# Weight splits in two-tile pieces, gate gemms over all levels, and smaller moves in a model of three blocks

## The reference, cut to what matters

```python
for l in range(2):                       # first model, 16 meta + 512 tokens, width 1024
    h = h + 0.5 * swiglu(rms_norm(h, ffn1_norm[l]), ffn1_w_gu[l], ffn1_w_down[l])
    u = rms_norm(h, mix_norm[l])
    c_q, c_kv, k_pe, hq, hf, hi, hg, ga, gb = split_cols(u @ w_in[l], IN_SPLITS)
    y_a = mla(c_q, c_kv, k_pe, ...) @ w_proj_attn[l]       # 8 heads, causal, with rope
    y_b = hgrn2(hq, hf, hi, hg, lbs[l], hg_norm[l]) @ w_proj_rec[l]   # 4 heads, gated recurrence
    merged = sigmoid(ga) * y_a + sigmoid(gb) * y_b
    h = h + merged @ w_out[l]
    h = h + 0.5 * swiglu(rms_norm(h, ffn2_norm[l]), ffn2_w_gu[l], ffn2_w_down[l])
x = rms_norm(h, final_norm)[:, 16:]
# second model, one layer, 512 tokens
u, q, k, v, qi, ki, wi, gates = split(rms(x) @ w_in_2)
y_ssm = s5(u)                            # complex diagonal recurrence, gelu, sigmoid gate
y_att = attention over the 256 keys that the indexer picks (top_k of qi, ki, wi)
x = x + (sigmoid(g_ssm) * (y_ssm @ w_proj_ssm) + sigmoid(g_att) * (y_att @ w_proj_attn)) @ w_out
x = x + (silu(h2 @ w_gate) * (h2 @ w_up)) @ w_down       # h2 = rms(x)
```

## Time and profile before

| | us |
|---|---|
| median of 3 runs | 3305.68 |
| lowest, highest | 3302.39, 3307.8 |
| profiled execution, its own time | 3303.59 |
| span of that execution's trace | 3301.8 |
| PE busy | 3218.9 (97%) |
| DVE, ACT, POOL busy | 1745.8, 1120.4, 1450.2 |

### The profile page before, as it was taken

One profiled execution on the slowest core, in us unless ns is written; L12 is line 12 of the kernel. 1 busy time (PEld: TensorE's weight loads), 2 busy tenths in 40 slices (PEclk: granted clock), 3 DMA queues, 4 the chain that ended last, 5 costly groups with the idle time before them and its releaser, 6 DMA issues.

```text
span 3301.8 us, 55446 instructions
## 1 busy us (share of the span) xinstructions
PE 3218.9 (97%) x21512; PEld 2916.4 (88%) x21512; DVE 1745.8 (53%) x2634; ACT 1120.4 (34%) x1590; POOL 1450.2 (44%) x661
## 2 busy tenths in 40 slices
PE   8999999999999999999999999999999999999999
PEld 7999988899999999999999888788888776788888
DVE  7363553477563546543662477633235678655434
ACT  4232433322342334332343222332324434243322
POOL 3564542122445655555642222444465442245555
PEclk9999999999999999999999999999999999999999
DMA  4333322133333333333332123333333433233333
GB/s 129 90 95 96 92 70 52 39 94 115 96 90 96 92 91 93 91 92 96 90 85 58 46 81 118 96 95 105 93 94 91 109 95 118 64 90 89 102 89 102
DMA packets 544860, 298.89 MB, mean 91 GB/s; under 512 B 23280, under 2 KB 528624, under 8 KB 544560
## 3 DMA queue, kind: packets, MB, share of 16 engines
q1 hardware_dynamic: 514128, 258.77, 27.6%
q10 hardware_dynamic: 30560, 37.72, 3.6%
HBM read 278.36 MB, written 16.91 MB: 89 GB/s over the span
## 4 chain that ended last, share of the span: by engine, by line
PE 61%; issue 25%; POOL 8%; DVE 4%; ACT 1%; DMA 1%; ACTq 0%; POOLq 0%; DVEq 0%; SPq 0%
PE pair L663 28%; PE pair L661 22%; PE aux L721 10%; POOL wl L526 6%; POOL SL L542 2%; DMA raw<-w_ffn_gate 0%; DVE tmp L1754 0%; PE aux L690 0%; ACTq L1513 0%; DVE negt L2244 0%; DVE top L2243 0%; DVE R L1702 0%; DVE R L1697 0%; DVE al L1757 0%; DVE R L2339 0%
## 5 line engine op out<-in xcount | busy, mean ns | idle before, releaser
L526 POOL TENSOR_TENSOR wl<-raw,wh 128x1024 fp32r<-128x1024 f32 (+4 forms) x513 | 1156.6, 2258 | 1812.5 <-ACT wh L1161 1610.5
L1161 ACT ACTIVATE wh<-raw 128x1024 fp32r<-128x1024 f32 (+4 forms) x513 | 490.2, 958 | 477.0 <-DMA raw<-ffn_w_down 152.8
L663 PE MATMUL pair<-xh,wh 128*128 128x264 f32 x2208 | 348.1, 291 | 18.9 <-DVE xl L1647 14.4
L1657 DVE SCALAR_TENSOR_TENSOR hT<-pair,hT 128x528 f32 (+3 forms) x144 | 100.8, 700 | 452.9 <-PE pair L663 258.9
L663 PE MATMUL pair<-xl,wh 128*128 128x264 f32 x2208 | 333.6, 285 | 0.0
L663 PE MATMUL pair<-xh,wl 128*128 128x264 f32 x2208 | 328.3, 285 | 0.0
L663 PEld LDWEIGHTS pair<-xh,wh 128*128 128x128 f32 x2208 | 295.5, 190 | 27.7 <-ACT wh L1161 9.3
L663 PEld LDWEIGHTS pair<-xl,wh 128*128 128x128 f32 x2208 | 295.3, 189 | 0.0
L663 PEld LDWEIGHTS pair<-xh,wl 128*128 128x128 f32 x2208 | 292.9, 189 | 0.0
L661 PE MATMUL pair<-xh,wh 128*128 128x512 f32 x920 | 255.5, 403 | 0.0
L661 PE MATMUL pair<-xl,wh 128*128 128x512 f32 x920 | 248.8, 395 | 0.0
(11 more groups left out here) (396 smaller groups left out, 5373.2 us busy)
## 6 DMA issues: line engine op xcount, KB each, us to landing
raw<-ffn_w_gu SPq DMA_DIRECT2D x176, 512.0 KB, 3.8
raw<-w_in SPq DMA_DIRECT2D x103, 512.0 KB, 3.9
raw<-ffn_w_down SPq DMA_DIRECT2D x64, 512.0 KB, 4.0
raw<-ffn_w_down SPq DMA_DIRECT2D x32, 384.0 KB, 3.5
raw<-w_out SPq DMA_DIRECT2D x24, 512.0 KB, 4.0
raw<-w_ffn_gate SPq DMA_DIRECT2D x22, 512.0 KB, 3.8
raw<-w_ffn_up SPq DMA_DIRECT2D x22, 512.0 KB, 3.9
gate_scratch<-gst ACTq DMA_DIRECT2D x32, 256.0 KB, 2.5
```

Source lines behind the costliest of these rows:

```text
L526: nc.gpsimd.tensor_tensor(wl[:, k % SPL, 0:n], raw[:, k % SPL, 0:n], wh[:, k % SPL, 0:n].bitcast(F32), ALU.subtract).then_inc(S["split_don ...
L663: mm = nc.tensor.matmul(pp[:, h, 0:th], wk, x[:, kk, t0 + h * th:t0 + (h + 1) * th], start=first, stop=last)
L1161: nc.scalar.activation(wh[:, k % SPL, 0:n], raw[:, k % SPL, 0:n], ACT.Copy).then_inc(S["split_hi"], 1)
L1657: v.scalar_tensor_tensor(halves(hm, T // 2), psum_pair(k, T // 2), factor, halves(hm, T // 2), ALU.mult, ALU.add).then_inc(S["evacuated"], 1)
```

## The change

It does seven things, on all engines. (1) GpSimd makes the low halves two k-tiles (256 columns) at a time in the gates, the projections, the output gemm and the second model's gemms, with one semaphore increment at the end as before. (2) The token sums of the FFNs are made a slot sooner: tile 0, then 1 and 2 in one slot, then 3. (3) The gate gemms stand at the levels of the table GATE_AT; its first entry is done in the tail of the attention (`first_gate`), its last after level 35, and with it the evacuation, the sigmoid, the store and the way back of all gates. (4) v turns begin behind two k-tiles of the first hgrn unit, and the tiles 2 to 4 stand within that unit; their banks are swapped; the rope copies are split over two slots. (5) The angles of chunk 0 stand ahead of the first gates on ScalarE and DVE, and three picks there are left to the attention's rounds. (6) The halves of the second attention's output are made for the tokens 0 to 383 at rounds 27 and 28, for the last 128 at the end. (7) In `v_turns` a wait for the probabilities' copies moves behind tile 0.

```diff
+        GATE_AT = (0, 3, 5, 7, 9, 11, 14, 16, 18, 20, 23, 25, 27, 30, 32, 35)
...
-            def split(l, k, kt, i=0):
-                n = kt * P
+            def split(l, k, kt, i=0, kp=None):
+
+                kp = kt if kp is None else kp
                 pool.wait_ge(S["split_hi"], U(l, k, i) + 1)
-                nc.gpsimd.tensor_tensor(wl[:, k % SPL, 0:n], raw[:, k % SPL, 0:n], wh[:, k % SPL, 0:n].bitcast(F32),
-                                        ALU.subtract).then_inc(S["split_done"], 1)
-
-            def run(l, k, kts, turns):
+                for k0 in range(0, kt, kp):
+                    n = slice(k0 * P, (k0 + kp) * P)
+                    ins = nc.gpsimd.tensor_tensor(wl[:, k % SPL, n], raw[:, k % SPL, n], wh[:, k % SPL, n].bitcast(F32), ALU.subtract)
+                ins.then_inc(S["split_done"], 1)
+
+            def run(l, k, kts, turns, kp=None):
                 with pool.Fori(0, turns) as i:
                     for j in range(4):
-                        split(l, k + j, kts[j], i)
+                        split(l, k + j, kts[j], i, kp)
...
-                run(l, U_GATE, [KD] * 4, 4)
-                run(l, U_PROJ, [4] * 4, 4)
-                run(l, U_WO, [KD] * 4, 2)
+                run(l, U_GATE, [KD] * 4, 4, 2)
+                run(l, U_PROJ, [4] * 4, 4, 2)
+                run(l, U_WO, [KD] * 4, 2, 2)
...
-            def v_turns(src, base):
-
-                for i, (st, sz) in enumerate(TT1):
+            def v_turns(src, base, tiles=range(len(TT1)), free=None):
+
+                for i in tiles:
+                    st, sz = TT1[i]
                     r = base + i
                     if i >= 2:
                         pe.wait_ge(S["vt_copied"], r - 1)
+                    if i == 1 and free is not None:
+                        pe.wait_ge(*free)
                     for j in range(4):
-                        mm = nc.tensor.transpose(bank[2 + i % 2][0:sz, j * 128:(j + 1) * 128], src(j, st, sz), ident)
+                        mm = nc.tensor.transpose(bank[3 - i % 2][0:sz, j * 128:(j + 1) * 128], src(j, st, sz), ident)
                     mm.then_inc(S["vt_done"], 1)
...
+                def v_tiles(*tiles):
+                    v_turns(lambda j, st, sz: vT[j][:, st:st + sz], l * 10, tiles)
+
+                def hg_slice(n, slot):
+                    if n == 1 and slot == 0:
+                        pe.wait_ge(S["vt_copied"], l * 10 + 5)
+                    for k, kt, kk in PLANS[l].parts[n][slot]:
+                        if n == slot == 0:
+                            if kk < 2:
+                                continue
+                            if kk in (4, 6):
+                                v_tiles(kk // 2)
+                        gemm(l, k, kt, (xh, xl), th, part=(kk,), alone=True)
+                        if n == slot == 0 and kk == KD - 1:
+                            v_tiles(4)
+                            pe.wait_ge(S["vt_copied"], l * 10 + 4)
+                t0, T = real(l)
+
+                def first_gate(x):
+                    if x == 0:
+                        pe.wait_ge(S["evacuated"], U(l, U_GATE) + PAIRS)
+                        gemm(l, U_GATE, KD, (xh, xl), T // 2, t0=t0)
                 pe.wait_ge(S["evacuated"], U(l, U_HG) + PAIRS)
-                v_turns(lambda j, st, sz: vT[j][:, st:st + sz], l * 10)
-
-                def hg_slice(n, slot):
-                    for k, kt, kk in PLANS[l].parts[n][slot]:
-                        gemm(l, k, kt, (xh, xl), th, part=(kk,), alone=True)
+                for kk in range(2):
+                    gemm(l, U_HG, KD, (xh, xl), th, part=(kk,), alone=True)
+                v_tiles(0, 1)
                 pe.wait_ge(S["rope_copied"], 3 * l + 3)
-                pe.wait_ge(S["vt_copied"], l * 10 + 5)
                 attention(at1[l], lambda h, st, sz: qT[:, h, st:st + sz], lambda h, c0, c1: kT[:, h, c0:c1],
                           lambda x, kn, h: vtok[0:kn, x, h * 64:h * 64 + 64], mask1,
-                          lambda n: hg_slice(n, 0), lambda n: hg_slice(n, 1))
-                pe.wait_ge(S["evacuated"], U(l, U_GATE) + PAIRS)
-                pe.wait_ge(at1[l].sem["pt_copied"], at1[l].n + at1[l].groups)
-                v_turns(lambda j, st, sz: hgv[j][:, st:st + sz], l * 10 + 5)
-
-                t0, T = real(l)
+                          lambda n: hg_slice(n, 0), lambda n: hg_slice(n, 1), first_gate)
+                v_turns(lambda j, st, sz: hgv[j][:, st:st + sz], l * 10 + 5, free=(at1[l].sem["pt_copied"], at1[l].n + at1[l].groups))
+
                 lv = 0
                 for i, (st, sz) in enumerate(TT1):
                     nl = sz.bit_length()
...
                                 lt, rt, n = kd[m % 2][:, h, 0:sz], qd[m % 2][:, h, 0:sz // 2], sz // 2
                             mm = nc.tensor.matmul(bank[lv % 2][0:sz, h * 128:h * 128 + n], lt, rt, start=True, stop=True)
                         mm.then_inc(S["lv_done"], 1)
-                        if lv == 0 or lv >= 3 and lv % 2 == 1 and lv // 2 < 2 * KD:
-                            gemm(l, U_GATE + lv // 2, KD, (xh, xl), T // 2, t0=t0)
+                        if lv in GATE_AT[1:]:
+                            gemm(l, U_GATE + GATE_AT.index(lv), KD, (xh, xl), T // 2, t0=t0)
...
-                            if early:
-                                kk = 2 * i + j
+                            for kk in ((0,), (1, 2), (3,), ())[2 * i + j] if early else ():
                                 w_thi(fs, kk, T // 2)
...
-                    for n in (1, 2) if j == 11 else ():
+                    for n in (j - 10,) if j in (11, 12) else ():
...
-                    while g < 2 * KD and 2 * g + 3 < lv:
+                    while g < 2 * KD - 1 and GATE_AT[g + 1] < lv:
                         gate(l, U_GATE, g, T, l)
                         g += 1
-                    if i == len(TT1) - 1:
-                        assert g == 2 * KD
-                        gates_back(l, U_GATE, T, gates2 if T == SEQ else gates1, l)
                     if i < len(TT1) - 1:
                         act.wait_ge(S["kht_done"], l * 4 + i + 1)
                         nc.scalar.activation(khT[0:sz, :, :], bank[3][0:sz, :].rearrange("p (h k) -> p h k", h=HG),
...
                         act.wait_ge(S["kq_ready"], l * 5 + i + 1)
                         for j in range(4):
                             nc.scalar.activation(ah[:, j, t0:T1], oT[:, j, t0:T1], ACT.Copy).then_inc(S["oth"], 1)
+                        assert g == 2 * KD - 1
+                        gate(l, U_GATE, g, T, l)
+                        gates_back(l, U_GATE, T, gates2 if T == SEQ else gates1, l)
...
+            angles(0)
             act.wait_ge(S["n2_ss"], 6)
             nc.scalar.activation(rq, bank[2][:, 0:32], ACT.Sqrt, bias=eps[:, 2:3]).then_inc(S["n2_rms"], 1)
             gates(0, EARLY)
-            angles(0)
...
+                if n == 27:
+                    act.wait_ge(at2.sem["pt_copied"], 29)
+                    nc.scalar.activation(ah[:, 0:4, 0:384], oT[:, :, 0:384], ACT.Copy).then_inc(S["oth"], 2)
...
-            for j in range(4):
-                nc.scalar.activation(ah[:, j, 0:SEQ], oT[:, j, 0:SEQ], ACT.Copy).then_inc(S["oth"], 1)
+            nc.scalar.activation(ah[:, 0:4, 384:SEQ], oT[:, :, 384:SEQ], ACT.Copy).then_inc(S["oth"], 2)
...
-                            w_tlo(fs, j - 1, th)
+                            w_tlo(fs, (0, 2, 3)[j - 1], th)
+                        if j == 1:
+                            w_tokens(fs, 1, T, own)
                         evac(l, k + 2 * j + 1, tm(US, T), rstd[:, 0:T], th)
                         dve.wait_ge(S["evacuated"], U(l, k + 2 * j + 1) + 1 + PAIRS)
                         activated(fi * FT + j, j)
-                        w_tokens(fs, j, T, own)
-                    if early:
-                        w_tlo(fs, 3, th)
+                        if j == 1:
+                            w_tlo(fs, 1, th)
+                        if j < 3:
+                            w_tokens(fs, (0, 2, 3)[j], T, own)
...
+                def v_copies(*tiles):
+                    for i in tiles:
+                        st, sz = TT1[i]
+                        dve.wait_ge(S["vt_done"], l * 10 + i + 1)
+                        v.tensor_copy(vtok[0:sz, i, :], bank[3 - i % 2][0:sz, :]).then_inc(S["vt_copied"], 1)
+                v_copies(0, 1)
...
-                    if lv >= 3 and lv % 2 == 1 and lv // 2 - 1 < 2 * KD:
-                        gate(l, U_GATE, lv // 2 - 1, T, l, rstd[:, t0:T1])
+                    if lv in GATE_AT[1:]:
+                        gate(l, U_GATE, GATE_AT.index(lv) - 1, T, l, rstd[:, t0:T1])
...
+                        gate(l, U_GATE, 2 * KD - 1, T, l, rstd[:, t0:T1])
...
+            angles(0, (0,))
             gates(0, 1)
             dve.wait_ge(S["n2_rms"], 3)
             v.reciprocal(rq, rq).then_inc(S["rq_ok"], 1)
             dve.wait_ge(S["rq_ok"], 1)
-            pick(3)
+            angles(0, (1,))
```

(9 more changed lines are left out.)

## The result

The changed kernel took 3314.55 us (median of 7 runs, 3312.94 to 3318.31), the kernel before 3302.92 in the same seven rounds: ratio 1.0036, 95% interval [1.0026, 1.0046], so 0.36% or some 12 us slower (9 to 15 by the interval). The profiled execution took 3314.55 us, its span is 3312.8 us.

The account below looks back on a forecast made before the run. PE, busy 97% of the span, was taken to bound the kernel, with its waits and half-clock stretches. Terms -14.0 - 2.3 + 0 + 16.2 + 2.5 + 8.4 - 1 - 2.0 - 3.5 = +4.3; 3303.6 + 4.3 + 2.1 = 3310.0 us, range 3286 to 3321.

Parts of the forecast that it names:

- Part 1: Four FFNs: token sums a slot sooner remove PE's waits for weights in the first combined groups, -14.0 us (-12 to -14).
- Part 2: v turns and first hgrn slices: two k-tiles ahead of the turns remove PE's waits for the last rotated tensor, -2.3 us.
- Part 3: First gate gemm in the attention tail: moves cover and adds none, 0 us (best -4, worst +3).
- Part 4: Gates over all levels, two layers: tile-start waits, later last gemm and gates' return, +16.2 us; slow clock after standing, +2.5.
- clock term of 8.4: Six token-tile starts: half clock after idle costs 1.4 us each, +8.4 us (0 to 18).
- Part 5: Low halves in 256-column pieces: POOL's work lengthens slightly, DVE is blocked for less, -1 us (-5 to +3).
- Rival D: POOL's pieces are held by DVE where PE awaits wl: +8.4 instead of -1, 3319.4 us; chance 0.04.
- Part 6: Chunk angles ahead of the gates: wait for the scan shrinks by 2.8, moved picks cost 0.8, -2.0 us.
- Part 7: Attention output: three quarters of the last low halves two rounds sooner, one wait left, -3.5 us (-1 to -5.5).
- C (the clock): Six tile starts: clock costs 3.1 us each instead of 1.4, total 3320.2 us; chance 0.14.
- A: Tile starts: clock stays at 2.4 GHz, total 3301.6 to 3299.1 us, down to 3294; chance 0.27.
- B: Tile starts or gates' return: new waits do not come, total 3285.7 us; chance 0.13.

Follow-up runs that it names:

- first_gate: Changed kernel with the first gate gemm still in the attention's tail, the other fifteen at odd levels 3 to 31, gates fetched as before: 3279.43 us, ratio 0.9930.
- no_gates: Changed kernel with gate gemms back at level 0 and odd levels from 3, none in the attention's tail, gates fetched as before: 3282.70 us, ratio 0.9935.
- best: more_pieces with the first gate gemm in the attention's tail: 3273.28 us, ratio 0.9904 to the kernel before.
- more_pieces: no_gates with FFN token sums one set a half slot, plus 256-column pieces in ordinary FFN tiles' and hgrn units: 3271.85 us, ratio 0.9905.
- filled: Changed kernel with the four products of each bare first level (token tiles 2 to 4, both layers) written three times: 3308.99 us, ratio 1.0020.
- pool_alone: Kernel before with only the low halves split in 256-column pieces: 3291.91 us, ratio 0.9962.
- out_ang: Kernel before with only chunk angles and picks moved and output halves made sooner: 3304.01 us, ratio 0.9999.
- best_filled: best with the products of levels 32 to 36 of each layer written twice into their bank: 3274.66 us, ratio 0.9912.

## Why the prediction was right, and where it was not

The forecast of 3310.0 against 3314.55 is the case that came, on the slow side. The gate part was foreseen in mechanism and in size. That the total came so near is partly luck. Against the kernel before I forecast +4.3 us, and some +12 came (+11.3 by the steps); the kernel before itself had a median 2.8 us lower in the seven rounds (3302.92) than the one I started from (3305.68). Two sizes were badly off, and they cancel in part.

- **Part 1 (-14.0) is the step that failed.** Measured -3.8 by the steps in the changed kernel; alone -2 by the runs and -4.7 in its trace. Of the 14.0 us of waits for weights 10.4 went, but 6.9 us of new waits for held evacuations came in the four FFNs. I costed only the chain to the weight sums, and not what the doubled slot puts ahead of the evacuation of the pair that PE needs next. That queue was in the diff: `w_tlo(1)` and `w_tokens(2)` follow each other ahead of the next slot's evacuation.
- **Part 2 (-2.3)**: -0.8 and +0.8 in the two layers, so nothing: the waits for HGT and HQ, 2.3 and 2.4 us before, are 2.5 and 3.6 us in the changed kernel, in front of the k-tiles now instead of in front of the turns. No run has this part alone.
- **Part 3 (0)**: first_gate against no_gates, and best against more_pieces, say 0.
- **Part 4 (+16.2, with +2.5 and +8.4 of clock: 27.1)**: 29.9 by the steps, 32 by no_gates. The new waits are right to a tenth: 2.0, 2.0, 1.6 and 2.0 a layer from matmul to matmul. The way back took longer than I took: 15.1 to 16.3 us to landing instead of 13.4, so the wait was 9.6 and 8.6, not 7.5. In layer 0 the last gate gemm ended at 804.56, the gates landed 21.4 us behind it (forecast 18.6) and the fourth projection gemm started 28.7 us behind it (forecast 23.5 without the clock). The clock term of 8.4 is 8.2 by the windows of the changed kernel, and filled, which had one such stretch left, gained 6.7 at the levels in its trace and 5 in its runs. But it came as three stretches of 3.4 to 6.8 us at three of the six starts, not as 1.4 at each.
- **Part 5 (-1)** was mis-sized: -12.6 alone, -10.4 in its trace. I looked for it where PE waits for POOL and at DVE in the levels, and not in the second model, where DVE sets the pace of S5, of the first attention rounds and of the output. The harm that its upper bound (+3) allowed for does come, but at one place: PE's waits for wl in WO rose from 2.8 to 3.6, which with the clock behind the longest costs 2.0 us in layer 1. Rival D doesn't come: a piece takes 0.85 us on the mean in pool_alone, where I took 0.77, so DVE holds POOL for less than 0.1 a piece.
- **Part 6 (-2.0)**: -2.6 in the changed kernel, 0 alone.
- **Part 7 (-3.5)**: -4.8 in the changed kernel, -3.7 alone. One wait of 1.6 is left, as forecast. The pieces alone give 2.5 at the same place, so the two overlap.
- **The 6.8 us between parts 6 and 7** were in no term. pool_alone has -5.6 there and out_ang +0.8, so they belong to part 5. Over all traces the stretch is 2.1 to 8.2 us shorter than in the kernel before where there are pieces, and from 2.3 us shorter to 3.6 longer where there are none.

By the steps in the changed kernel part 1 was 10.2 us worse than forecast, part 4 2.8 and part 2 2.3, while part 5 in the second model was 5.8 better and parts 3, 6 and 7 together 2.5: 7.0 us in all, the difference of +11.3 and +4.3. That part 5 made up for more than half of part 1 was no merit of the sum. Of the rivals, C (the clock) was the right mechanism at the size of the forecast; A and B didn't come: the clock fell, and the waits were all there.

The Trainium skill ("SBUF — State Buffer", who interferes with whom) gives the rule for part 5, that the pair of ports is held for a whole instruction; the 2.59 us of TL at 55.09, and the mean of 871 ns that fell to 575 with pieces, agree with it.

## What to carry to other kernels

Where two engines block each other for whole instructions, cut the long instruction of the one that has time: it pays where the other one sets the pace, which need not be where the first is waited for. Then mind the places where that unit is awaited itself, since in pieces it ends later. A filler (here a gemm) that moves off a place bares it: list what each one covered, the chain that it hid and the store or load that its result sets off, before moving it; the last one of a row decides when the row's result comes back. And when a slot takes more work on an engine that also frees another's buffers, ask first which release stands behind it.

## What was not expected of the hardware

The clock did not follow the busy time of PE alone: in best_filled it fell behind 2.76 busy us of 3.40, all 64-column products, and stayed at 0.50 through 6.72 of 6.80; in filled it stayed at 1.00 through 2.03 of 3.40 (743.0 to 746.4), which came behind a dense row of 128-column products; in the changed kernel it fell behind 1.10 and 1.62 of 3.40. These are single executions. The transfer that brings the gates back took 13.1 to 13.6 us in the kernel before and 15.1 to 16.3 us in the changed one, with the same size and shape. It goes with the place: in the four kernels that fetch late it took 14.8 to 16.4 us, in the ten others 13.0 to 14.4. What it meets there was not tried.
